# Reciprocals written as full rows and turned in one pass, in place of small reciprocals spread by fp32 products

## The chip, the cores and the metric

The kernel runs on one core of one Trainium2 chip. The metric is the device time of one execution, in microseconds (us). A change is read against the median of several executions of the kernel before.

## The reference, cut to what matters

The reference runs a convolution layer, a gated linear attention layer and a second block on a sequence of 1024 tokens and 1024 channels. Two places matter here.

The convolution mixer normalises over channels before its gate (`layer_norm` of `c`):

```python
mu = jnp.mean(xf, axis=-1, keepdims=True)
xc = xf - mu
var = jnp.mean(xc * xc, axis=-1, keepdims=True)
y = xc * lax.rsqrt(var + LN_EPS) * g + b
```

The second block has a causal attention with a softmax over keys, 8 heads of 64 channels, in blocks of 128 query rows:

```python
scores = jnp.einsum('bqhd,bkhd->bhqk', q_i, k).astype(jnp.float32) * scale
scores = scores + c_i[:, :, :, None] - c[:, :, None, :]
probs = jax.nn.softmax(scores, axis=-1).astype(v.dtype)
return jnp.einsum('bhqk,bkhd->bqhd', probs, v)
```

The kernel divides by the softmax's sum after the last product, not before it.

## The kernel before, in words

The kernel is written with explicit semaphores. Each engine (PE for products, DVE for VectorE, ACT, POOL, SP for loads) runs its own list of instructions in the written order, stage after stage, and waits where a semaphore is not yet at its count. Activations lie in SBUF with channels on the partitions and tokens along the row, so a number that belongs to a token or to a query row has to be made the same on all partitions before it can multiply such a tile.

**The attention stage** (functions `attn_tensor`, `attn_scalar`, `attn_vector`, `attn_pool`) goes over 8 turns. A turn is a block of 128 query rows; the first turn has the last block (1024 keys), the last turn the first block (128 keys). Each turn has 8 heads, worked on in 4 pairs, so there are 32 pairs `p`, and one step of the loop serves pair `p` on PE together with older pairs. In a step, in order:

- PE: `scores(p)` (L2043) writes both heads' scores to PSUM; at the second step of the next turn `spread` (L2099); in the steps 20 to 31 two early products of the output projection (L2032, L2030; the list `FILL_AT`); `turn_probs(2p-2)` (L2072, one transpose for each block of 128 keys); `values(p-2)` (L2085); `turn_probs(2p-1)`; at the second step of a turn `pooled` (L2108).
- DVE: `reduce(2p)` (L2227, adds the decay to the scores and takes the row's minimum; it waits for `scores(p)`), `keep(2p-2)` (L2237, copies the second half of the turned probabilities out of PSUM), `reduce(2p+1)`, at the first step of the next turn `sums` (L2242), `keep(2p-1)`, at the second step `leave` (L2248, L2251).
- ACT: `leave(2p-2)` (L2167, copies the first half of the turned probabilities), at the second step `keep_spread` (L2173), two `probs` (L2054, the exponential, whose accumulator gives the row's sum), `leave(2p-1)`, and some larger casts.

`turn_probs(s)` waits until the first `s` probabilities have been copied out of PSUM by ACT (`prob_left`) and by DVE (`prob_kept`), since all use the same two banks.

**The row sums.** The exponentials of a turn leave 8 sums for each query row in 8 columns of the tile `stat`. DVE inverts them in place (`sums`, L2242, 128x8). PE then makes each of the 8 columns into 64 equal rows (`spread`, L2099): an fp32 product whose stationary operand is the column repeated 64 times and whose moving operand is the identity. The result in PSUM bank 7 has channels on partitions and query rows along the row. ACT copies it to `sums_bc` (L2173) and DVE multiplies the attention output with it (L2248). PE's list has `spread` right behind `scores(p)` and ahead of the early products and `turn_probs(2p-2)`.

**The deviations.** After the convolution the tokens are in four chunks. For the chunks 1 to 3 PE sums the squares, turns the sums into columns of `stat`, ACT takes the root, DVE inverts the 1 or 3 columns (`inverse`, L785), and `variance_spread` (L773) makes each column into a 128x128 block by an fp32 product with the identity: 7 in all. DVE multiplies with that block (L799). Around it PE runs products that are already possible (L956, L967), and ACT runs roots (L838) and, after the last root, a table load and the SiLUs (L844).

In the code below `at(name, shape, offset, type)` names a region of SBUF; two names may share a region.

Of the kernel before, what the change touches and what calls it, by code (L numbers as in the profile page):

```python
# [8 lines left out]
F32R = mybir.dt.float32r  # L9
I32 = mybir.dt.int32  # L10

P = 128
# [7 lines left out]
HALF = 512  # L20
# [11 lines left out]
AH, AD = 8, 64  # L32
# [39 lines left out]
def hybrid_block(nc, I, out):  # L72
    ctx = ExitStack()
    with ctx:
        base = (nc.sbuf_base + 31) // 32 * 32

        def at(name, shape, off, dt=F32):
            return nc.alloc_sbuf_tensor_at(name, shape, dt, offset=base + off)
# [5 lines left out]
        C0 = 0  # L84
# [6 lines left out]
        Z0 = O0 + KT * T * 4  # L91

        ident_r = at("ident", [P, P], C0, F32R)
# [134 lines left out]

        PS = ctx.enter_context(nc.psum_tensor("PS", [P, 8, 512], F32))

        x_stage_t = at("x_stage_t", [P, 4, D], O0, F32R)
        silu_z_t = at("silu_z_t", [P, KT, T], O0, F32R)
        rows3_t = [silu_z_t[:, :, c:c + P] for c in (400, 528, 656)]
# [494 lines left out]
        def stat_bank(place, c):  # L728
            bank, c0 = place[c]
            return PS[:, bank, c0:c0 + CHUNKS4[c][1]]  # L730
# [39 lines left out]
        def variance_spread(pe, c):  # L770
            pe.wait_ge(centered, RSTD_LEFT[c])
            for b in range(CHUNKS4[c][1] // P):
                last = nc.tensor.matmul(stat_bank(VAR_AT, c)[:, b * P:(b + 1) * P], VAR_COLS(c)[:, b:b + 1].broadcast_to([P, P]), ident[:],  # L773
                                        start=True, stop=True)
            last.then_inc(var_ready, 1)

        def part_left(dve, c):
# [1216 lines left out]
        def row_sums(turn):  # L1994
            return stat[:, 60 + 8 * (turn % 2):68 + 8 * (turn % 2)]

        def block_cols(i):
            return slice(i * P, (i + 1) * P)
# [58 lines left out]
        def attn_tensor(pe):  # L2057
            pe.wait_ge(f_split, 4 + 2)
            pe.wait_ge(v6_left, 4 + 2 * NX)

            def scores(p):
                pair_rows(pe, p)

            def turn_probs(s):
                i, _, _ = step(s)
                a = first_blocks(i)
                pe.wait_ge(prob_ready, s + 1)
                after(pe, prob_left, s)
                after(pe, prob_kept, min(s, SPLIT))
                for kb in range(i + 1):  # L2070
                    b = kb if kb < a else 4 + kb - a
                    last = nc.tensor.transpose(blocks(4)[:, b, :].bitcast(F32R), score_t_of(s)[:, block_cols(kb)], ident_r[:])  # L2072
                last.then_inc(prob_turned, 1)

            def values(p):

                i, turn, h0 = step(2 * p)
                pe.wait_ge(prob_left, 2 * p + 2)
                pe.wait_ge(prob_kept, min(2 * p + 2, SPLIT))
                if h0 == 0 and turn > 0:  # L2080
                    pe.wait_ge(tail_dve, of_turn(turn - 1, ATTN_LEFT))
                for kb in range(i + 1):
                    for e in range(2):
                        h = h0 + e
                        ins = nc.tensor.matmul(PS[e * AD:(e + 1) * AD, 6, block_cols(h0 // 2)], v6[:, kb, h * AD:(h + 1) * AD],  # L2085
                                               prob_t[(2 * p + e) % 4][:, block_cols(kb)], start=kb == 0, stop=kb == i)
                        if kb == i:
                            ins.then_inc(pv_done, 1)

            def spread(turn):  # L2090

                pe.wait_ge(tail_dve, of_turn(turn, SUMS))
                if turn > 0:
                    pe.wait_ge(tail_dve, of_turn(turn - 1, POOL_LEFT))
                if turn > 1:
                    pe.wait_ge(tail_act, of_turn(turn - 1, SS_LEFT))
                for h in range(AH):
                    out = PS[h % 2 * AD:(h % 2 + 1) * AD, 7, block_cols(h // 2)]
                    last = nc.tensor.matmul(out, row_sums(turn)[:, h:h + 1].broadcast_to([P, AD]), ident[:], start=True, stop=True)  # L2099
                last.then_inc(tail_pe, 1)  # L2100

            def pooled(turn):
                if turn == 0:
                    pe.wait_ge(gain_in, G6 + 64)
                    pe.wait_ge(pool_ready, 4)
                pe.wait_ge(tail_act, of_turn(turn, SPREAD_LEFT))
                for g in range(4):
                    last = nc.tensor.matmul(quarter(7)[:, g, :], w_pool[:, g, :], pool_u[:, g, block_cols(row_of(turn))],  # L2108
                                            start=True, stop=True)
                last.then_inc(tail_pe, 1 if turn > 0 else 2)  # L2110

            for p in range(PAIRS + 2):
                if 0 < p < PAIRS:
                    scores(p)
                if turn_at(p, 1) is not None:
                    spread(turn_at(p, 1))
                if p in FILL_AT:
                    if p == FILL_AT[0]:
                        pe.wait_ge(w_low, 4)
                        pe.wait_ge(x_low, 1)  # L2120
                    n = 2 * (p - FILL_AT[0])
                    for e, k, m in ROW_TERMS[n:n + 2]:
                        mix_product(0, e, k, m, 1)
                if 1 <= p <= PAIRS:
                    turn_probs(2 * p - 2)
                if p >= 2:
                    values(p - 2)
                if 1 <= p <= PAIRS:
                    turn_probs(2 * p - 1)
                if turn_at(p, 1) is not None:  # L2130
                    pooled(turn_at(p, 1))
                if turn_at(p, 2) is not None and turn_at(p, 2) > 0:
                    square_sums(pe, turn_at(p, 2) - 1)
# [83 lines left out]
        def attn_vector(dve):  # L2217
            dve.wait_ge(cum_in, 16)

            def reduce(s):  # L2220
                i, _, h = step(s)
                n = (i + 1) * P
                dve.wait_ge(score_done, s + 1)
                dve.wait_ge(mask_done, s + 1)
                after(dve, prob_turned, s - 3)

                nc.vector.tensor_tensor_reduce(score_of(s)[:, 0:n], cum_bc[:, h, 0:n], banks(2 * (s % 2), 2, n), 1.0, BIG,  # L2227
                                               ALU.add, ALU.min, low_score(s)).then_inc(score_ready, 1)

            def keep(s):  # L2230
                i, _, _ = step(s)
                a, n = first_blocks(i) * P, (i + 1) * P
                if i == 0:
                    return
                dve.wait_ge(prob_turned, s + 1)
                after(dve, pv_done, 2 * (s // 2 - 1))
                nc.vector.tensor_copy(prob_t[s % 4][:, a:n], PS[:, 5, 0:n - a]).then_inc(prob_kept, 1)  # L2237

            def sums(turn):

                dve.wait_ge(prob_ready, (turn + 1) * AH)
                nc.vector.reciprocal(row_sums(turn), row_sums(turn)).then_inc(tail_dve, 1)  # L2242

            def leave(turn):
                cols = block_cols(row_of(turn))
                dve.wait_ge(tail_act, of_turn(turn, SPREAD_LEFT))
                dve.wait_ge(pv_done, (turn + 1) * AH)
                nc.vector.tensor_tensor(mix_t[:, 0:4, cols], quarter(6), sums_bc[:].rearrange("p (k q) -> p k q", k=4), ALU.mult)\  # L2248
                    .then_inc(tail_dve, 1)
                dve.wait_ge(tail_pe, of_turn(turn, POOLED))  # L2250
                nc.vector.tensor_tensor(mix_t[:, 4:8, cols], quarter(7),  # L2251
                                        pool_gain[:].rearrange("p (k o) -> p k o", o=1).broadcast_to([P, 4, P]), ALU.mult)\
                    .then_inc(tail_dve, 1)

            for p in range(PAIRS + 2):
                if p < PAIRS:
                    reduce(2 * p)
                if 1 <= p <= PAIRS:
                    keep(2 * p - 2)
                if p < PAIRS:  # L2260
                    reduce(2 * p + 1)
                if turn_at(p, 0) is not None:
                    sums(turn_at(p, 0))
                if 1 <= p <= PAIRS:
                    keep(2 * p - 1)
                if turn_at(p, 1) is not None:
                    leave(turn_at(p, 1))
                if turn_at(p, 2) is not None and turn_at(p, 2) >= 4:
                    weights_low(dve, nc.vector, turn_at(p, 2))
            weights_low(dve, nc.vector, NX - 1)  # L2270
# [1012 lines left out]
```

## Time and profile before

| | us |
|---|---|
| median of 3 runs | 2139.09 (2138.34 to 2140.31) |
| time of the profiled execution | 2136.45 |
| its span in the profile | 2134.7 |
| PE busy | 2104.7 (99% of the span) |
| DVE busy | 1267.3 (59%) |
| ACT busy | 810.6 (38%) |
| POOL busy | 1035.2 (48%) |

The span runs from the first to the last instruction of the profiled execution; its time is 1.75 us longer. PE is busy nearly all the time by this count, which takes a matmul from its issue to its modelled end, so the count hides short waits. The attention stage lies at about 1114 to 1250 us, and the deviations are spread at 314 to 326 us.

### The profile page before, as it was taken

How to read it: one execution, taken by the hardware profiler on the slowest of the kernel's cores; microseconds unless marked ns; L12 is line 12 of the kernel's file. 1: busy time of each engine (PE TensorE's matmuls, PEld its weight loads, DVE VectorE, ACT ScalarE, POOL GpSimd, SP SyncE). 2: the span in 40 equal slices, each digit the busy share in tenths (PEclk: the TensorE clock that was granted, in tenths of full speed). 3: DMA queues.
4: the chain of work that ended last, by engine and by line, in shares of the span. 5: the costliest groups of instructions: out<-in, count | busy, mean ns of one | idle time of the engine just before them, and what ended most of it. 6: DMA issues, size and time to landing. Idle time of an engine off the chain costs nothing.

```text
span 2134.7 us, 31643 instructions
## 1 busy us (share of the span) xinstructions
PE 2104.7 (99%) x12176; PEld 1820.7 (85%) x12176; DVE 1267.3 (59%) x1674; ACT 810.6 (38%) x1324; POOL 1035.2 (48%) x723
## 2 busy tenths in 40 slices
PE   8999999999999999999999999999999999999999
PEld 8999977899999998888787778888888888888787
DVE  4899988900049976640016645866656666666854
ACT  3454554112158852210226754432222222222453
POOL 3789941142256745022295630265556556555700
PEclk9999999999999999999999999999999999999999
DMA  4111123411100024221302022111111111111421
GB/s 162 41 40 40 61 79 90 127 56 40 41 21 1 1 82 146 89 70 40 119 1 85 2 99 109 50 47 52 49 59 55 44 49 59 59 39 49 178 72 56
DMA packets 128729, 136.65 MB, mean 64 GB/s; under 512 B 7054, under 2 KB 113294, under 8 KB 128492
## 3 DMA queue, kind: packets, MB, share of 16 engines
q1 hardware_dynamic: 128620, 135.11, 19.2%
q8 instruction: 79, 1.29, 0.2%
q14 instruction: 30, 0.25, 0.0%
HBM read 118.29 MB, written 16.81 MB: 63 GB/s over the span
## 4 chain that ended last, share of the span: by engine, by line
PE 82%; DVE 7%; POOL 4%; issue 3%; ACT 3%; DMA 1%; POOLq 0%; SPq 0%; ACTq 0%; DVEq 0%
PE PS L390 43%; PE PS L2700 18%; PE PS L2032 4%; POOL side_sum L622 2%; PE PS L2043 2%; PE PS L2085 2%; PE PS L2413 2%; PE PS L1323 1%; PE PS L1356 1%; PE PS L2072 1%; PE PS L440 1%; POOL wl L366 1%; PE PS L429 1%; PE PS L1741 1%; ACT glu L844 1%
## 5 line engine op out<-in xcount | busy, mean ns | idle before, releaser
L2899 DVE TENSOR_TENSOR ff_acc<-ff_acc,PS 128x512 f32<-128x512 f32 x320 | 216.4, 685 | 185.4 <-PE PS L390 184.8
L390 PE MATMUL PS<-xh,wh 128*128 128x352 f32 (+2 forms) x944 | 288.2, 337 | 1.3 <-ACT silu_z L577 1.1
L390 PE MATMUL PS<-xl,wh 128*128 128x352 f32 (+2 forms) x944 | 286.5, 335 | 0.0
L390 PE MATMUL PS<-xh,wl 128*128 128x352 f32 (+2 forms) x944 | 285.9, 334 | 0.0
L2615 POOL TENSOR_TENSOR xl<-raw,xh 128x512 fp32r<-128x512 f32 x120 | 164.6, 1380 | 136.6 <-ACT xh L2752 136.6
L674 DVE SCALAR_TENSOR_TENSOR PS<-glu,conv_vec,PS 128x1040 f32<-128x1040 f32 (+2 forms) x196 | 228.5, 1236 | 1.1
L390 PE MATMUL PS<-wh,xh 128*128 128x256 f32 (+1 forms) x712 | 207.9, 316 | 1.5 <-ACT r_silu L1629 0.6
L390 PE MATMUL PS<-wl,xh 128*128 128x256 f32 (+1 forms) x712 | 206.8, 314 | 0.0
L390 PE MATMUL PS<-wh,xl 128*128 128x256 f32 (+1 forms) x712 | 206.4, 314 | 0.0
L390 PEld LDWEIGHTS PS<-xh,wh 128*128 128x128 f32 x944 | 175.2, 189 | 9.4 <-issue 1.3
L390 PEld LDWEIGHTS PS<-xl,wh 128*128 128x128 f32 x944 | 175.0, 188 | 8.0
L390 PEld LDWEIGHTS PS<-xh,wl 128*128 128x128 f32 x944 | 174.9, 188 | 7.7
L371 POOL CAST wh<-raw 128x2048 fp32r<-128x2048 f32 x15 | 28.5, 1897 | 294.7 <-PE PS L390 142.9
L2752 ACT CAST xh<-raw 128x512 fp32r<-128x512 f32 x120 | 72.4, 619 | 238.2 <-PE PS L2700 141.6
L366 POOL TENSOR_TENSOR wl<-raw,wh 128x2048 fp32r<-128x2048 f32 x29 | 134.3, 4631 | 26.3 <-ACT wh L362 25.1
L390 PEld LDWEIGHTS PS<-wh,xh 128*128 128x128 f32 x712 | 132.7, 188 | 11.2 <-ACT v_meta L1234 1.1
L390 PEld LDWEIGHTS PS<-wh,xl 128*128 128x128 f32 x712 | 134.1, 188 | 9.1
L390 PEld LDWEIGHTS PS<-wl,xh 128*128 128x128 f32 x712 | 133.8, 188 | 9.2
L2607 POOL TENSOR_TENSOR raw<-raw 128x512 f32<-128x512 f32 x80 | 115.2, 1441 | 50.7 <-DMA raw<-in_w_ffn_up_dram 44.7
L390 PE MATMUL PS<-dnh,ffh 128*128 128x512 f32 x336 | 131.1, 390 | 0.3 <-ACT ff_acc L2763 0.3
L390 PE MATMUL PS<-dnh,ffl 128*128 128x512 f32 x336 | 130.8, 389 | 0.0
L390 PE MATMUL PS<-dnl,ffh 128*128 128x512 f32 x336 | 130.8, 389 | 0.0
(456 smaller groups left out, 4944.9 us busy)
## 6 DMA issues: line engine op xcount, KB each, us to landing
rows<-h_rows SPq DMA_DIRECT2D x24, 512.0 KB, 3.3
dn_raw<-in_w_ffn_down_dram SPq DMA_DIRECT2D x22, 512.0 KB, 3.5
raw<-in_gla_w_in_dram SPq DMA_DIRECT2D x10, 1024.0 KB
raw<-in_w_ffn_gate_dram SPq DMA_DIRECT2D x20, 512.0 KB
raw<-in_w_ffn_up_dram SPq DMA_DIRECT2D x20, 512.0 KB
raw<-in_conv_w_in_dram SPq DMA_DIRECT2D x16, 512.0 KB, 7.1
raw<-in_w_in_dram SPq DMA_DIRECT2D x8, 1024.0 KB
h_rows<-rows SPq DMA_DIRECT2D x16, 512.0 KB, 2.6
```

The lines of the kernel that those rows point to most:

```text
L366: nc.gpsimd.tensor_tensor(wl[slot][:], raw_of(u)[0][:], wh[slot][:].bitcast(F32), ALU.subtract).then_inc(unit_ready, 1)
L390: last = nc.tensor.matmul(out_of(c, cn), s, x[:, c0:c0 + cn], start=n == 0 and m == 0, stop=n == len(terms) - 1 and m == 2)
L622: ins = nc.gpsimd.tensor_tensor(acc[:], acc[:], tap_part[n % 3][:], ALU.add)
L674: ins = nc.vector.scalar_tensor_tensor(out=y, in0=x, scalar=w, in1=y, op0=ALU.mult, op1=ALU.add)
L2032: return nc.tensor.matmul(out, x, w[:, k, cols], start=begin, stop=end)
L2043: ins = nc.tensor.matmul(PS[:, 2 * e + c0 // 512, 0:cn], aqk[rows, k, i * P:(i + 1) * P], aqk[rows, 4 + k, c0:c0 + cn], start=True, stop=True)
L2085: ins = nc.tensor.matmul(PS[e * AD:(e + 1) * AD, 6, block_cols(h0 // 2)], v6[:, kb, h * AD:(h + 1) * AD], prob_t[(2 * p + e) % 4][:, block ...
L2607: nc.gpsimd.tensor_tensor(out, a, b, op).then_inc(pool_own.sem, 1)
L2615: nc.gpsimd.tensor_tensor(lo, OP_AT[o], hi.bitcast(F32), ALU.subtract).then_inc(unit_ready, 1)
L2700: ins = nc.tensor.matmul(PS[:, OP_BANK[o], :], s[:, k, :], x[:, k, :], start=k == 0 and m == 0, stop=k == 3 and m == 2)
L2752: nc.scalar.copy(ring(o)[0], OP_AT[o]).then_inc(unit_hi, 1)
L2899: nc.vector.tensor_tensor(x, x, PS[:, dn_bank(p, n), :], ALU.add).then_inc(dn_left, 1)
```

## The change

Three edits.

1. Two more names are given to existing regions, as fp32r: `stat_t` for `stat`, and `sums_bc_t` for `sums_bc`.
2. `variance_spread` uses a transpose of the repeated column in fp32r, into the same PSUM block, where it had an fp32 product with the identity. The seven blocks stay.
3. `sums` no longer inverts 128x8 in place. It reads each of the 8 sums 64 times and writes the inverses as a full row of 512 columns into `sums_bc`. `spread` then turns the four 128x128 blocks of that row with four transposes, where it had eight fp32 products. ACT's copy, DVE's product and the order of all lists stay.

```diff
+        stat_t = at("stat_t", [P, 96], C0 + 2272, F32R)
+        sums_bc_t = at("sums_bc_t", [P, HALF], Z0 + 32768, F32R)
...
         def variance_spread(pe, c):
             pe.wait_ge(centered, RSTD_LEFT[c])
             for b in range(CHUNKS4[c][1] // P):
-                last = nc.tensor.matmul(stat_bank(VAR_AT, c)[:, b * P:(b + 1) * P], VAR_COLS(c)[:, b:b + 1].broadcast_to([P, P]), ident[:],
-                                        start=True, stop=True)
+                col = 20 + 4 * c + b
+                last = nc.tensor.transpose(stat_bank(VAR_AT, c)[:, b * P:(b + 1) * P].bitcast(F32R), stat_t[:, col:col + 1].broadcast_to([P, P]), ident_r[:])
             last.then_inc(var_ready, 1)
...
-                for h in range(AH):
-                    out = PS[h % 2 * AD:(h % 2 + 1) * AD, 7, block_cols(h // 2)]
-                    last = nc.tensor.matmul(out, row_sums(turn)[:, h:h + 1].broadcast_to([P, AD]), ident[:], start=True, stop=True)
+                for q in range(AH // 2):
+                    last = nc.tensor.transpose(PS[:, 7, block_cols(q)].bitcast(F32R), sums_bc_t[:, block_cols(q)], ident_r[:])
                 last.then_inc(tail_pe, 1)
...
             def sums(turn):
 
                 dve.wait_ge(prob_ready, (turn + 1) * AH)
-                nc.vector.reciprocal(row_sums(turn), row_sums(turn)).then_inc(tail_dve, 1)
+                nc.vector.reciprocal(sums_bc[:].rearrange("p (h n) -> p h n", n=AD),
+                                     row_sums(turn).rearrange("p (h o) -> p h o", o=1).broadcast_to([P, AH, AD])).then_inc(tail_dve, 1)
```

## Rows read from the trace of the kernel before

**Rows 1.** The page: busy time of PE and DVE, and the chain that ended last.
```profile
PE 2104.7 (99%) x12176; PEld 1820.7 (85%) x12176; DVE 1267.3 (59%) x1674; ACT 810.6 (38%) x1324; POOL 1035.2 (48%) x723
...
PE 82%; DVE 7%; POOL 4%; issue 3%; ACT 3%; DMA 1%; POOLq 0%; SPq 0%; ACTq 0%; DVEq 0%
```

**Rows 2.** Busy time by stretch: PE, PEld, DVE, ACT, POOL, then granted clock.
```profile
1134.00:1155.00 21.00, 21.00 (x227) 15.66 (x225) 13.46 (x27) 14.57 (x27) 18.25 (x17) 1.00 0.06 24
1221.00:1233.00 12.00, 12.00 (x111) 8.84 (x111) 7.70 (x29) 9.06 (x30) 7.09 (x10) 1.00 0.01 1
```

**Rows 3.** Groups by shape on DVE: reciprocals, and one copy.
```profile
L2493 DVE RECIPROCAL stat<-stat 128x1 f32<-128x1 f32 x8 | 1.3, 164 | 11.6 <-ACT stat L2457 11.6
L2242 DVE RECIPROCAL stat<-stat 128x8 f32<-128x8 f32 x8 | 1.6, 198 | 1.3 <-ACT score L2054 1.3
L1636 DVE RECIPROCAL stat<-stat 128x32 f32<-128x32 f32 x1 | 0.4, 353 | 1.3 <-ACT stat L1617 1.3
L796 DVE RECIPROCAL PS<-PS 128x144 f32<-128x144 f32 x1 | 1.1, 1067 | 0.0
L2237 DVE COPY prob_t<-PS 128x512 f32<-128x512 f32 x8 | 5.5, 687 | 1.8 <-PE PS L2072 1.8
```

**Rows 4.** Timeline around the first turn's spread: start, duration, engine, line.
```profile
1134.78 0.20 DVE L2242 RECIPROCAL stat<-stat 128x8 f32<-128x8 f32 x1
1135.68 0.69 DVE L2237 COPY prob_t<-PS 128x512 f32<-128x512 f32 x1 [0.70 <-PE PS L2072]
1137.27 0.85 PEld L2099 LDWEIGHTS PS<-ident,stat 128*64 128x64 f32 x16 [0.55 <-issue]
1137.38 1.09 DVE L2227 CUSTOM_DVE_ANT_0 score<-cum_bc,PS 128x896 f32<-128x896 f32 x1 [1.01 <-PE PS L2043]
1138.30 0.66 PEld L2072 LDWEIGHTS PS<-ident,score_t 128*128 128x128 f32 x7 [0.17 <-issue]
1141.57 1.12 PE L2108 MATMUL PS<-pool_u,w_pool 128*128 128x128 f32 x8
```

**Rows 5.** Timeline, four transposes in a row and PE's next load.
```profile
1201.05 0.40 PEld L2072 LDWEIGHTS PS<-ident,score_t 128*128 128x128 f32 x4 [0.17 <-issue]
1201.39 0.52 PEld L2014 LDWEIGHTS PS<-ones_mean,sq_sum 128*128 128x128 f32 x4
```

**Rows 6.** Timeline, fourth, fifth, seventh and eighth turn: reciprocal, and what follows the spread.
```profile
1192.56 0.20 DVE L2242 RECIPROCAL stat<-stat 128x8 f32<-128x8 f32 x1
1195.35 0.39 PEld L2072 LDWEIGHTS PS<-ident,score_t 128*128 128x128 f32 x4 [0.17 <-issue]
1207.68 0.20 DVE L2242 RECIPROCAL stat<-stat 128x8 f32<-128x8 f32 x1
1210.12 0.19 PEld L2032 LDWEIGHTS PS<-mo_h,xl 128*128 128x128 f32 x1 [0.17 <-issue]
1233.52 0.20 DVE L2242 RECIPROCAL stat<-stat 128x8 f32<-128x8 f32 x1
1235.42 0.19 PEld L2032 LDWEIGHTS PS<-mo_h,xh 128*128 128x128 f32 x1 [0.17 <-issue]
1242.72 0.20 DVE L2242 RECIPROCAL stat<-stat 128x8 f32<-128x8 f32 x1 [1.31 <-ACT score L2054]
1245.69 0.59 ACT L2173 COPY sums_bc<-PS 128x512 f32<-128x512 f32 x1
1246.33 2.08 PE L2108 MATMUL PS<-pool_u,w_pool 128*128 128x128 f32 x8 [0.25 <-ACT sums_bc L2173]
```

**Rows 7.** Busy time and granted clock by stretch, end of the attention stage.
```profile
1242.00:1244.00 2.00, 0.87 (x6) 0.45 (x6) 0.20 (x1) 2.00 (x8) 1.76 (x3) 1.00 0.00 0
1244.00:1246.00 2.00, 1.89 (x21) 1.52 (x21) 0.00 (x0) 1.53 (x4) 2.00 (x1) 0.75 0.00 0
1246.00:1248.00 2.00, 1.75 (x10) 1.67 (x9) 0.69 (x1) 0.28 (x1) 0.22 (x1) 0.50 0.36 94
```

**Rows 8.** Timeline around the spread of the third chunk's deviations.
```profile
318.44 0.74 PEld L773 LDWEIGHTS PS<-ident,stat 128*128 128x128 f32 x6 [0.62 <-issue]
319.19 0.74 PEld L767 LDWEIGHTS PS<-ones_mean,var_part 128*128 128x128 f32 x6
320.25 1.28 ACT L844 ACT_TABLE_LOAD   x1
```

## The prediction, made before the changed kernel ran

> **What bounds the kernel now.** I read the page first: PE is busy 99% of the span and holds 82% of the chain that ended last; DVE is busy 59% and holds 7% of that chain [rows 1]. So time that PE gains or loses should count nearly one for one, and DVE's counts only where PE waits for it. The views by stretch say the same of the attention stage: in the stretch around the first turn's spread PE is busy 21.00 of 21 us and DVE 13.46, and in a late one 12.00 of 12 and 7.70 [rows 2]. DVE thus has some 35% of idle time there. But the timeline shows that this idle time is in pieces of 0.70 and 1.01 us between instructions that PE needs soon [rows 4], and DVE runs its list in order. The question is what one long DVE instruction does in the place of the small reciprocal.
>
> **The price of the long reciprocal.** The trace has no reciprocal of 512 columns, but it has 128x1 at 164 ns, 128x8 at 198, 128x32 at 353 and 128x144 at 1067 [rows 3]. From 1 to 32 columns this is 189/31 = 6.1 ns a column, from 32 to 144 it is 714/112 = 6.4. A copy of 512 columns takes 687 ns, 1.3 ns a column [rows 3]; the reciprocal is plainly not one column a cycle. The engine has to make 512 results even if each input is read 64 times. At 6.35 ns I get 1.07 + 368 x 0.00635 = 3.40 us, against 0.20 now: 3.2 us more on DVE in each of 8 turns. Bounds: 0.69 (the copy) and, with the steeper slope, 3.45; I take 3.40, since four points lie on one line.
>
> The Trainium skill (VectorE: DVE Perf Modes, "First, the fixed hardware budget") says that a reciprocal runs an iterative divide with a repeat count of 8. Taken as 8 cycles of 0.96 GHz a column that would be an estimated 8.3 ns and 4.4 us; the rows show about 6 cycles (6.35 ns), and they decide, but the direction is the same and speaks against a repeated input.
>
> **The price of the new spread on PE.** Now: 16 weight loads (two for each of the 8 products) from 1137.27, and the next loads at 1138.30, a slot of 1.03 us [rows 4]. Four transposes in a row hold PE 0.34 us to its next load [rows 5]; I take 0.40. Were the row ready in time, each turn would gain 0.62 us.
>
> **Where the long reciprocal lies in a turn.** It is issued at 1134.78 and would end at 1138.18, while PE wants it at 1137.27 [rows 4]. Behind it on DVE stand the copy `keep` of the old turn's last head (0.69 us) and the next `reduce`. PE waits for the reciprocal in `spread`, and behind it PE's `turn_probs` waits for that copy (`prob_kept`). First turn: copy ends at about 1134.78 + 3.32 + 0.69 = 1138.79, 0.05 for the signal, so the transposes start at 1138.84 where they started at 1138.30: +0.54. The other path, 1138.18 + 0.05 + 0.40 = 1138.63, is shorter. `reduce` starts 1.3 us later than now, at about 1138.7, and ends before ACT gets to its exponential, which stands behind PE's transposes in any case, so nothing more is added. Everything after shifts by the same amount, since each engine follows PE here.
>
> The turns get shorter (fewer keys), so the cover shrinks. Fourth turn: 1192.56 + 3.45 + 0.40 = 1196.41 against 1195.35, +1.06. Fifth: 1207.68 + 3.85 = 1211.53 against the early product at 1210.12, +1.41. Seventh: 1233.52 + 3.85 = 1237.37 against 1235.42, +1.95. Eighth: the reciprocal ends at 1246.12, the transposes reach PSUM some 0.5 us later, and ACT's copy starts at about 1246.65 against 1245.69, +0.96 [rows 6]. The second, third and sixth turn I put between their neighbours: 0.71, 0.89, 1.68. Sum: 0.54 + 0.71 + 0.89 + 1.06 + 1.41 + 1.68 + 1.95 + 0.96 = +9.2 us. PE's saving of 0.62 us a turn is already in it, since I compared starts behind the spread. POOL and SP get no new wait; their work lies behind events that shift with PE.
>
> **The deviations.** The slot of three spreads is 318.44 to 319.19, 0.75 us for 6 loads [rows 8]. Three transposes at 0.09 hold 0.27, so 0.48 less; a single one saves some 0.17. The first two spreads (one block, three blocks) stand ahead of the last root on ACT and thus of the table load at 320.25 that the SiLUs wait for; the third (0.48) lies among PE's products. DVE's reciprocal of these columns is not changed. I take -0.6 (0.17 + 0.48), with -1.2 (all three count) and 0 (DVE's later work there absorbs it) as ends.
>
> **The clock.** At the end of the attention stage PE is busy 0.87 of 2 us, then the granted clock falls to 0.75 and 0.50, the lower of the two levels, 1.2 GHz for 2.4 [rows 7]. There the eight `pooled` products take 2.08 us [rows 6] where they took 1.12 in the first turn [rows 4]. In the changed kernel PE idles about 2 us or more for the reciprocal in the fifth, sixth and seventh turn. I expect the clock to fall in one or two of these, at about 1 us each by that row (0.96): +1.2, with 0 and +4 as ends.
>
> The Trainium skill (TensorE: Matmul & The Clock Gate, Part 4) says that transposes do not count as activity for the clock. That would make the falls likelier, since the new spread is transposes where the old one was products; no row here separates the two.
>
> **Sum.** 9.2 - 0.6 + 1.2 = +9.8 us. The profiled execution (2136.45) would become about 2146.3; it is 2.6 us under the median of the runs, so for the median I give 2139.1 + 9.8 = 2148.9 us, 0.46% slower. No change that a measurement of this kernel can tell is about 0.2%, 4.3 us.
>
> **The rivals.**
> - The row costs what a copy costs (on the other side: faster). If the chip makes the repeated results at 1.3 ns a column, the reciprocal takes 0.69 us, is ready before PE wants it in every turn, and the change gives 8 x -0.62 - 0.6 = -5.6: 2133.5. For it: only that the input is the same 8 numbers. Against: the four reciprocal rows. It turns at about 2.25 us for the reciprocal (3.40 less the mean loss of 9.2/8), 4.1 ns a column. Chance 0.05.
> - The reciprocal is hidden by DVE's idle time. For it: 35% of DVE idle. Against: the copy and the spread behind it are both waited for by PE within 2.5 us in the first turn and 0.9 in the seventh. If PE had other slack that gives back most of it, +1 to +4: 2140 to 2143. Chance 0.05. A weaker form, +4.3 to +7 (2143.4 to 2146), because later waits of PE take up part: 0.08.
> - The clock falls in four or more turns, or the repeated input makes the divide dearer. Five falls: 9.2 - 0.6 + 5 = +13.6, 2152.7; a divide one us longer would give 8 more, 2157. For it: the idle times grow turn by turn. Against: no row has such short gaps with a fall but the one. Chance 0.12.
> - The forecast, +7 to +13: 0.70.
>
> **How the numbers follow.** Range 2145.0 to 2153.5: it leaves out the faster and the hidden case (0.10), some of the weaker form, and the dearest clock or divide. Faster by over 0.2%: 0.05; within 0.2%: 0.05; slower: 0.90.
>
> **What the profile of the changed kernel would show.** L2242 as 128x512 at 3.3 to 3.5 us, eight times. L2099 (under its new line number) with 4 loads a turn in 0.35 to 0.4 us. PE idle before it 0.9 us in the first turn, growing to 2.5 in the seventh, with DVE's reciprocal as the releaser. The spread of the deviations with 7 loads and not 14. The granted clock below 1.00 in some stretch between 1205 and 1240. The forecast is wrong if the reciprocal takes under 2.3 us, if PE's idle time before the spread does not grow, or if the end of the attention stage does not shift by about 9 us.

## The result, and the profile of the changed kernel

The changed kernel takes 2152.57 us (median of 4 runs, 2151.73 to 2153.59), the kernel before beside it 2138.72 us (4 runs, 2136.66 to 2140.31). The ratio is 1.0067 with a 95% interval of 1.0054 to 1.0080: 13.85 us slower, where +9.8 was forecast. The profiled execution has a span of 2150.0 us against 2134.7, 15.3 more.

First the page of the changed kernel, the busy time and the chain that ended last:

```profile
PE 2106.9 (98%) x12073; PEld 1821.5 (85%) x12073; DVE 1289.4 (60%) x1674; ACT 810.3 (38%) x1324; POOL 1035.0 (48%) x723
...
PE 76%; DVE 8%; POOL 8%; issue 4%; ACT 3%; DMA 1%; SPq 0%; POOLq 0%; DVEq 0%; ACTq 0%
```

DVE has 22.1 us more work than in [rows 1], 60% of the span against 59%; PE's busy time barely moves, and of the chain PE still has 76%, against 82%. The busy times would let one believe that nothing happened. The view of the reciprocal's line and of its instructions says otherwise (durations are minimum, median and maximum in ns; "who waited" is in us and times):

```profile
L2243 DVE RECIPROCAL sums_bc<-stat x8: 3347/3348/3353, 1134.9 to 1255.8; 128x512 f32<-128x512 f32 x8
...
  PEld PS L2100: 16.4, 8
  PE PS L2100: 13.0, 8
```

Each of the eight takes 3.35 us, and each time PE waits for it: PE idles for 13.0 us in front of the new transposes. The timeline of the first turn, and then the transposes of the fourth to eighth turn (start, duration; in brackets the engine's idle time and who ended it):

```profile
1134.89 3.35 DVE L2243 RECIPROCAL sums_bc<-stat 128x512 f32<-128x512 f32 x1
...
1138.16 0.63 DVE L2238 COPY prob_t<-PS 128x512 f32<-128x512 f32 x1
1138.30 0.39 PEld L2100 LDWEIGHTS PS<-ident,sums_bc_t 128*128 128x128 f32 x4 [1.45 <-DVE sums_bc L2243]
1138.30 0.53 PE L2100 MATMUL PS<-ident,sums_bc_t 128*128 128x128 f32 x4 [0.83 <-DVE sums_bc L2243]
1138.70 1.07 DVE L2228 CUSTOM_DVE_ANT_0 score<-cum_bc,PS 128x896 f32<-128x896 f32 x1
1138.90 0.65 PEld L2074 LDWEIGHTS PS<-ident,score_t 128*128 128x128 f32 x7 [0.22 <-issue]
...
1197.88 0.54 PE L2100 MATMUL PS<-ident,sums_bc_t 128*128 128x128 f32 x4 [1.57 <-DVE sums_bc L2243]
...
1213.94 0.53 PE L2100 MATMUL PS<-ident,sums_bc_t 128*128 128x128 f32 x4 [1.91 <-DVE sums_bc L2243]
...
1230.76 0.53 PE L2100 MATMUL PS<-ident,sums_bc_t 128*128 128x128 f32 x4 [2.16 <-DVE sums_bc L2243]
...
1245.61 0.75 PE L2100 MATMUL PS<-ident,sums_bc_t 128*128 128x128 f32 x4 [2.46 <-DVE sums_bc L2243]
...
1255.82 3.35 DVE L2243 RECIPROCAL sums_bc<-stat 128x512 f32<-128x512 f32 x1 [1.30 <-ACT score L2056]
1259.23 0.75 PE L2100 MATMUL PS<-ident,sums_bc_t 128*128 128x128 f32 x4 [1.77 <-DVE sums_bc L2243]
```

In [rows 4] the spread's slot lay from 1137.27 to 1138.30, and the next loads began at 1138.30. Now the transposes only begin there, hold PE for 0.60 us up to the next transposes at 1138.90, and these begin 0.60 later. The idle time before the spread grows from 0.83 us in the first turn to 2.46 in the seventh, as the turns get shorter. The same four transposes, 0.53 or 0.54 us in the first six turns, take 0.75 in the last two: PE's clock is down. The views by stretch show where (duration; busy us of PE, PEld, DVE, ACT, POOL; granted clock; DMA):

```profile
1206.00:1210.00 4.00, 4.00 (x41) 2.93 (x42) 2.85 (x9) 3.67 (x11) 3.92 (x8) 1.00 0.01 2
1210.00:1214.00 4.00, 2.09 (x23) 1.23 (x19) 4.00 (x5) 1.62 (x6) 2.68 (x2) 1.00 0.00 0
1214.00:1218.00 4.00, 4.00 (x29) 3.28 (x30) 1.38 (x6) 2.06 (x6) 0.91 (x2) 0.57 0.02 4
...
1226.00:1230.00 4.00, 2.60 (x24) 1.74 (x24) 3.54 (x6) 2.48 (x8) 3.74 (x5) 1.00 0.00 0
1230.00:1234.00 4.00, 3.24 (x23) 2.63 (x24) 1.81 (x7) 1.74 (x6) 0.91 (x2) 0.70 0.00 0
...
1244.00:1248.00 4.00, 2.39 (x13) 1.86 (x15) 2.10 (x6) 0.52 (x2) 0.66 (x1) 0.66 0.00 0
1248.00:1252.00 4.00, 4.00 (x21) 3.12 (x18) 1.89 (x6) 2.10 (x7) 0.00 (x0) 0.50 0.01 2
```

A stretch with PE busy 2.09 of 4 us is followed by one at 0.57; 2.60 is followed by one at 0.70; the third time the clock stays down for longer. In the kernel before there is one such fall in the stage, at its end [rows 7].

To see where the 15.3 us come from I took the starts of the reciprocals, which mark the turns. Before: 1134.78, 1156.09, 1175.53, 1192.56, 1207.68, 1221.73, 1233.52, 1242.72. After: 1134.89, 1156.68, 1176.68, 1194.47, 1210.53, 1227.36, 1242.20, 1255.82. The difference of the intervals is what a turn lost; the last one runs to the end of the span (891.98 and 894.18 us).

| turn | 1 | 2 | 3 | 4 | 5 | 6 | 7 | 8 | sum |
|---|---|---|---|---|---|---|---|---|---|
| lost, us | 0.48 | 0.56 | 0.76 | 0.94 | 2.78 | 3.05 | 4.42 | 2.20 | 15.2 |
| forecast without the clock | 0.54 | 0.71 | 0.89 | 1.06 | 1.41 | 1.68 | 1.95 | 0.96 | 9.2 |

The first four turns are as forecast, each 0.06 to 0.15 us under it. The last four lost 12.45 where 6.0 was forecast: these are the turns in which the clock is down. The rest, 0.1 us, lies ahead of the first turn, where the deviations should have given 0.6; but single executions scatter by more than that there. In the executions shown below the first turn's reciprocal starts anywhere from 1134.38 to 1137.75, so the views of turns are compared by their intervals, and the deviations by a view of their own.

### The profile page after: what moved, and what is told of

The parts are those of the page before. It is cut to its first block, busy times and chain, and to the rows that moved or that the text cites. A ratio compares the mean times of both kernels' runs of the same rounds, so it can differ in the third digit from the quotient of the medians.

```text
span 2150.0 us, 31437 instructions
## 1 busy us (share of the span) xinstructions
PE 2106.9 (98%) x12073; PEld 1821.5 (85%) x12073; DVE 1289.4 (60%) x1674; ACT 810.3 (38%) x1324; POOL 1035.0 (48%) x723
## 4 chain that ended last, share of the span: by engine, by line
PE 76%; DVE 8%; POOL 8%; issue 4%; ACT 3%; DMA 1%; SPq 0%; POOLq 0%; DVEq 0%; ACTq 0%
PE PS L392 40%; PE PS L2702 18%; PE PS L2034 3%; POOL side_sum L624 2%; PE PS L2415 2%; PE PS L1325 1%; PE PS L1358 1%; PE PS L442 1%; POOL wl L368 1%; DVE sums_bc L2243 1%; PE PS L431 1%; PE PS L1743 1%; POOL pool_tmp L2288 1%; PE PS L2087 1%; ACT glu L846 1%
## 5 line engine op out<-in xcount | busy, mean ns | idle before, releaser
L676 DVE SCALAR_TENSOR_TENSOR PS<-glu,conv_vec,PS 128x1040 f32<-128x1040 f32 (+2 forms) x196 | 228.4, 1232 | 1.1
```

Of the source, the lines that this page charges most:

```text
L676: ins = nc.vector.scalar_tensor_tensor(out=y, in0=x, scalar=w, in1=y, op0=ALU.mult, op1=ALU.add)
```

## The experiments

My theory: the loss is the time that PE waits for the long reciprocal, and in the short turns PE's clock falls on top. Rivals: the deviations cost or give something; the transposes are the dearer part; the clock is a small term, and something else makes the late turns dearer. All kernels compute the whole reference. Those with filler make, besides, fp32 products of the identity with itself whose result nobody reads: each is two loads and two matmuls, and eight in a row hold PE's loads for 1.86 us, 0.23 us each.

**One part of the change each.** `e1_conv_alone` has only the new `variance_spread`, `e2_attn_alone` only the long reciprocal and the transposes in `spread`.

> Only the deviations' spread is changed; the attention stage is as before. Theory A (the gain goes into a new wait): the seven transposes take half the loads, but PE's next product behind the third chunk's spread waits for VectorE's copy of the next chunk's partial sums, so the time stays within 1 us of before. Theory B (the forecast's step): PE's list ahead of the last root gets shorter by 0.6 us and the kernel with it, 2138.1. Theory C: the deviations carry part of the loss, 1 us or more slower.

> Only the attention edit, the deviations' spread as before. Theory A: the whole loss is here, +13 to +15 us. Rival: part of it comes from the deviations or from an interplay of both, then +11 us or less.

Measured beside a median before of 2137.79: 2137.49 for the deviations alone, ratio 0.9996 (0.9987 to 1.0005), and 2152.39 for the attention alone, 1.0064 (1.0051 to 1.0078). The whole loss is the attention part, and the deviations bring nothing that shows; by itself the interval, from -2.8 to +1.1 us, would leave room for the forecast 0.6. The timeline decides it. First the deviations alone, then the kernel before:

```profile
318.89 0.29 PEld L776 LDWEIGHTS PS<-ident,stat_t 128*128 128x128 f32 x3 [0.62 <-issue]
...
319.03 0.56 DVE L783 COPY var_part<-PS 128x384 f32<-128x384 f32 x1 [1.08 <-PE PS L763]
...
319.64 0.74 PEld L769 LDWEIGHTS PS<-ones_mean,var_part 128*128 128x128 f32 x6 [0.46 <-DVE var_part L783]
...
328.85 0.73 PE L392 MATMUL PS<-wh,xh 128*128 128x512 f32 x2 [0.68 <-DVE xl L812]
```

```profile
318.58 0.56 DVE L781 COPY var_part<-PS 128x384 f32<-128x384 f32 x1 [1.07 <-PE PS L761]
...
328.39 0.73 PE L390 MATMUL PS<-wh,xh 128*128 128x512 f32 x2 [0.26 <-DVE xl L810]
```

The three transposes do hold PE for only 0.29 us, but the next loads still begin 0.75 us after them, exactly the slot of [rows 8]. The gap is now a wait for DVE's copy of `var_part`, which ends at 319.59. In the kernel before that copy ends at 319.14, 0.05 us ahead of the same loads: PE's work filled the time, and what PE saved it now waits. The last spread does give PE some 0.4 us, but behind it PE waits for DVE's `xl`, 0.68 us where it waited 0.26, and that product starts 0.46 us later than before, as did the work ahead of the deviations (0.4 us).

`e2_attn_alone` also shows that the falls of the clock are not tied to certain turns. Its fourth turn has the same idle time of 1.57 us before the transposes as the changed kernel's, and there the clock falls (the two views are its transposes and its stretch of 4 us behind them):

```profile
1198.72 0.55 PE L2100 MATMUL PS<-ident,sums_bc_t 128*128 128x128 f32 x4 [1.57 <-DVE sums_bc L2243]
```

```profile
1202.00:1206.00 4.00, 4.00 (x30) 2.95 (x31) 2.82 (x7) 1.95 (x4) 0.37 (x1) 0.78 0.02 4
```

Turn by turn it lost 0.48, 0.57, 0.75, 2.43, 2.81, 3.06, 3.08 and, up to the end of the span, 1.76 us: 14.9 in all, as much as the changed kernel, otherwise divided.

**A small reciprocal, and the row by a copy.** `e3_small_reciprocal_then_copy` keeps the four transposes and leaves out the slow form:

```
-                nc.vector.reciprocal(<row of 512>, <8 sums, each read 64 times>).then_inc(tail_dve, 1)
+                dve_own.step(dve, nc.vector.reciprocal(row_sums(turn), row_sums(turn)))
+                nc.vector.tensor_copy(<row of 512>, <8 sums, each read 64 times>).then_inc(tail_dve, 1)
```

> The reciprocal is 128x8 in place as before, then VectorE copies it to the full row, and PE turns the row with the four transposes. Theory A (the loss is the long reciprocal alone, and the four transposes by themselves are worth 0.6 us a turn): the copy takes 0.3 to 0.7 us and is done before PE wants it in every turn, so the kernel gets faster than before by 8 x 0.6 = 4.8 us, 2134. Rival (the transposes cost more than they look, for instance through the clock): same as before or slower. The middle case, 2137 to 2139: in the late turns the copy comes just too late.

Measured: 2139.14, ratio 1.0004 (0.9995 to 1.0013). The loss is gone, so it was the long reciprocal and not the transposes; but there is no gain either, where theory A had 2134. The first three turns each take 0.7 us less than before (intervals 20.61, 18.77, 16.34 against 21.31, 19.44, 17.03), which is the slot saved; the sixth and seventh take 0.46 and 1.22 more, and from the eighth reciprocal to the end of the span it is 1.09 more, with the clock at 0.84, 0.50 and 0.80 in the stretches from 1244, 1248 and 1252. (`dve_own.step` makes DVE wait for its own small reciprocal.) The view of the copy's line, and its timeline in the first and the seventh turn:

```profile
L2244 DVE COPY sums_bc<-stat x8: 426/1815/2508, 1137.7 to 1245.2; 128x512 f32<-128x512 f32 x8
```

```profile
1137.67 0.43 DVE L2244 COPY sums_bc<-stat 128x512 f32<-128x512 f32 x1
...
1234.62 2.35 POOL L2309 TENSOR_TENSOR xl<-mix_t,xh 128x1024 fp32r<-128x1024 f32 x1
...
1234.74 2.51 DVE L2244 COPY sums_bc<-stat 128x512 f32<-128x512 f32 x1
...
1237.30 0.22 PEld L2100 LDWEIGHTS PS<-ident,sums_bc_t 128*128 128x128 f32 x2 [2.05 <-DVE sums_bc L2244]
```

The same copy takes 0.43 us alone and 2.51 beside an instruction of POOL; it ends 0.28 us after POOL's does. In the fourth to sixth turn it is the same beside the making of `xl` (1.78 to 2.06 us), and in the second beside that of `mix_sq` (1.85): each time the copy ends 0.27 to 0.29 us after POOL's instruction. In all of these POOL's instruction had begun first. In the eighth turn the copy began first, 0.02 us ahead of the making of `sq_sum`; there it took 0.43 us, and POOL's instruction 0.99 where the same one took 0.72 to 0.79 in the other turns. So by these rows the one that begins later waits. The long reciprocal shows nothing of the kind, 3347 to 3353 ns in all turns, with POOL making `xl` beside it in most of them, in the fourth and fifth turn begun ahead of it. The Trainium skill (GPSIMD Engine Reference, "Specifications") says that GpSimd shares its SBUF interfaces with VectorE and collides with its instructions in a 2-port mode or with two SBUF inputs; VectorE: DVE Perf Modes ("Mode 2×_2P") says that copies from SBUF to SBUF are among the operations that can use such a mode. The trace agrees that the two collide, 0.43 against 2.51; no run here shows that the mode is the reason.

**The row by ACT.** `e5_row_made_by_act`: the small reciprocal, and ACT copies the row, behind its last copy of the old turn.

```
+            def make_row(turn):
+                act.wait_ge(tail_dve, of_turn(turn, SUMS))
+                nc.scalar.copy(<row of 512>, <8 inverse sums, each read 64 times>).then_inc(row_made, 1)
```

> Reciprocal 128x8 in place on VectorE, ScalarE copies it to the full row behind its last copy of the step, four transposes on PE. Theory A (the four transposes are worth 0.6 to 0.7 us a turn wherever the row is there in time, and VectorE's copy was late only because it stretched beside GpSimd's long instructions): ScalarE's copy takes 0.6 us in every turn. It is in time in the first five turns and up to 0.7 us late in the last, so the kernel gets 2 to 4 us faster than before, 2134 to 2136. Rival: ScalarE's own queue is pushed back and gives the gain back, same as before. It would be the first version that beats both kernels.

> The kernel of the fifth run again beside the two others, to tell its small gain from none: -1.8 us if the first measurement holds, 0 if it was the scatter.

Measured: 2135.49 beside 2137.28, ratio 0.9993 (0.9984 to 1.0002); the second time 2134.87 beside 2137.02, 0.9992 (0.9983 to 1.0001). Both medians are lower, by 1.8 and 2.2 us, and neither interval excludes no change. ACT's copy in the first and the seventh turn, and PE's loads behind it:

```profile
1136.38 0.62 ACT L2173 COPY sums_bc<-stat 128x512 f32<-128x512 f32 x1
...
1137.25 0.39 PEld L2101 LDWEIGHTS PS<-ident,sums_bc_t 128*128 128x128 f32 x4 [0.54 <-ACT sums_bc L2173]
...
1231.08 2.37 POOL L2315 TENSOR_TENSOR xl<-mix_t,xh 128x1024 fp32r<-128x1024 f32 x1
...
1231.86 0.63 ACT L2173 COPY sums_bc<-stat 128x512 f32<-128x512 f32 x1
...
1232.55 0.22 PEld L2101 LDWEIGHTS PS<-ident,sums_bc_t 128*128 128x128 f32 x2 [0.83 <-ACT sums_bc L2173]
```

ACT's copy takes 0.61 to 0.64 us in all turns, beside POOL's making of `xl` too. In the first turn it ends at 1137.00 and PE's matmuls run through; in the seventh PE waits for it. Turn by turn the intervals are 0.70, 0.69, 0.08, 0.46, 0.42 and 0.18 us shorter than before, and 0.03 longer in the seventh: 2.5 us in seven turns, not 7 x 0.62 = 4.3. From the eighth reciprocal to the end of the span it takes 0.92 us more than before, which eats more than a third of that; the granted clock is 0.50 from 1242 to 1248 us.

**How much is the clock?** `e4_long_reciprocal_pe_kept_busy` and `e6_filler_cut_to_the_gap` are the changed kernel with filler in front of PE's wait for the row in the last five turns, so that PE doesn't idle there; the first has 10, 13, 15, 17 and 14 products, the second 5, 7, 8, 9 and 6.

```
+                if turn >= 3:
+                    for n in range(WARM[turn]):
+                        nc.tensor.matmul(PS[:, 7, 0:P], ident[:], ident[:], start=True, stop=True)
                 pe.wait_ge(tail_dve, of_turn(turn, SUMS))
```

> The changed kernel, but in the turns 4 to 8 PE runs 10 to 17 small fp32 products of the identity into the same PSUM bank ahead of its wait for the reciprocal; the spread overwrites their result. Theory A (of the loss of 13.9 us some 6 us are the clock that falls after PE's idle time): the granted clock stays at 1.00 in the turns 5 to 7 and the kernel is 4 to 6 us faster than the changed one, +8 to +10 over before. Rival 1 (the waits alone make the loss, the clock is a side effect): no gain, +13 to +15. Rival 2: the filler itself delays the spread, and it is slower than the changed kernel.

> The changed kernel with the filler of the run before cut to the idle time measured in the changed kernel: 5, 7, 8, 9 and 6 products at 0.25 us in the turns 4 to 8, where it had 10 to 17, which overshot the gap. Theory A (the clock's falls cost some 5 to 6 us of the 13.9): the clock stays at 1.00 from 1206 to 1245 us, the fifth to seventh turn lose 1.4, 1.6 and 1.9 us and no more, and the kernel comes to +8.5 to +10 over before. Rival (the falls cost nothing by themselves): +13 to +14, with the clock up.

The first took 2152.53 beside 2137.79, ratio 1.0066 (1.0053 to 1.0080): nothing won. Its clock is 1.00 in the stretches of 4 us from 1206, 1214, 1232 and 1244, but the filler ran on beyond the gap: its 17 products of the seventh turn hold PE for 4.06 us, where the gap was 2.46. Its fourth to seventh turn are 1.58, 2.23, 2.69 and 3.11 us longer than before, and the eighth, up to the end of the span, 3.60. What the clock costs cannot be read from it. The second took 2145.95 beside 2137.28, ratio 1.0038 (1.0025 to 1.0052), 8.7 us over its base where the attention part alone was 14.6 over its own. Its stretches:

```profile
1214.00:1218.00 4.00, 3.85 (x40) 3.28 (x39) 2.72 (x9) 2.10 (x7) 0.93 (x2) 1.00 0.01 4
1232.00:1236.00 4.00, 4.00 (x34) 3.14 (x36) 3.00 (x10) 3.34 (x13) 1.26 (x3) 1.00 0.00 0
1244.00:1248.00 4.00, 3.92 (x32) 2.63 (x30) 2.17 (x7) 3.02 (x10) 0.00 (x0) 1.00 0.03 6
1252.00:1256.00 4.00, 3.64 (x21) 3.55 (x21) 2.33 (x1) 1.65 (x6) 2.36 (x1) 0.57 0.00 0
```

The clock stays up except at the very end, and the turns lose 0.46, 0.56, 0.76, 0.94, 1.33, 1.55, 1.88 and, up to the end of the span, 0.95 us, 8.4 in all. The first four are those of the changed kernel, and the last four are what was forecast without the clock. So the falls cost 6.8 us by the turns (15.2 - 8.4), and by the medians 5.9 against the attention part alone (14.6 - 8.7) or 5.2 against the changed kernel (13.85 - 8.67). The slowest run with this filler, 2146.77, is 3.98 us under the fastest of `e2_attn_alone`, 2150.75.

**The long row in the first four turns only.** `e7_long_row_in_first_four_turns` goes back to the products of the kernel before in the last four.

> The long reciprocal and the four transposes in the first four turns alone, the small reciprocal and the eight products in the last four. Theory A (the loss grows as the turns get shorter, by cover and by clock): +2.5 to +3.5 us, a fifth of the whole loss. Rival (each turn loses the same): half of it, +7.

Measured: 2138.53 beside 2137.28, ratio 1.0005 (0.9996 to 1.0014). Its first four intervals are 21.78, 20.01, 17.79 and 16.08 us, 2.76 more than before in all, and the next three 14.04, 11.79 and 9.19, as before. Here a turn with the long row harms no later one; no fall of the clock came in the fourth turn of this execution. The median moved by 1.25 us; 2.76 is still within the interval, so this run fixes the price of four turns by its trace alone.

**Filler in the last turn.** In the last turn the kernel before has a fall of its own [rows 7]. `e8_before_with_filler_in_last_turn` puts 3 and 2 products ahead of the last two `turn_probs`; `e9_row_by_act_and_filler` does the same, with 3 more ahead of the last spread, in the kernel in which ACT makes the row.

> The kernel before, with five small products of the identity in the last step of the attention stage (three ahead of its first turn of probabilities, two ahead of its second), into a PSUM bank that is idle there. Theory A (the fall of the clock at the end of the stage comes from PE's two idle gaps of 0.8 us and costs 1.5 to 2 us): the granted clock stays at 1.00 from 1244 to 1248 us and the kernel is 1.5 to 2 us faster, 2135.5. Rival (the fall costs nothing, or the filler delays what it stands before): same as before or slower.

> The version with ScalarE's row (fifth run) and the same filler, with three more products ahead of the last spread. Theory A: both gains add, 2 us of the row and 1.5 to 2 us of the clock, 2133.5 to 2134, clear of the kernel before. Rival: the row's copy on ScalarE is what the last turn waits for, and the filler brings nothing there, -2.

Measured beside 2137.02: 2135.76, ratio 0.9993 (0.9984 to 1.0002), and 2134.06, 0.9982 (0.9972 to 0.9991). The stretches of the second:

```profile
1240.00:1244.00 4.00, 3.97 (x33) 3.00 (x30) 0.71 (x5) 3.52 (x12) 2.90 (x3) 1.00 0.00 0
1244.00:1248.00 4.00, 3.33 (x25) 2.65 (x24) 1.58 (x3) 2.03 (x4) 1.47 (x1) 1.00 0.31 86
```

The clock no longer falls there, in either of the two. By itself that is 1.3 us, too little to be told from nothing by its interval; in the trace the time from the eighth reciprocal to DVE's next one behind the stage (1253.31 before, 1251.74 here) is 1.1 us shorter than before, and to the end of the span 0.7. Where ACT makes the row the same filler shortens the time from the eighth reciprocal to the end of the span by 1.9 us (891.04 against the 892.90 of `e5_row_made_by_act`). This is the one version that is clearly faster than the kernel before, by 3.0 us between the medians and by 0.18% in the ratio, and the one with the lowest median of all that ran; `e10_row_made_by_act_again`, measured beside it, is 0.8 us above it, with runs that overlap.

## Why the prediction was right, and where its sizes were off

- **The direction and the mechanism** were right: a long DVE instruction in front of a product that PE wants soon, repeated eight times. `e2_attn_alone` carries the loss alone, and `e3_small_reciprocal_then_copy`, with the same transposes, doesn't have it. The size was not: the forecast proper, +7 to +13 us, missed 13.85.
- **The price of the reciprocal**: 3.40 us forecast, 3.35 measured. The line through four shorter rows [rows 3] held out to 512 columns: (3.348 - 1.067)/368 is 6.2 ns a column, not the 6.35 assumed. Reading each sum 64 times makes it no cheaper; the copy's price as a lower bound is refuted. The measured 6.2 ns speak against the 8.3 ns that the prediction estimated from the Trainium skill (VectorE: DVE Perf Modes, "First, the fixed hardware budget").
- **The slot of the spread**: 0.40 us forecast, up to the next loads 0.60 in the first turn, since those wait for the copy `prob_kept` behind the reciprocal; this is the gate that the prediction took for the first turn (1138.84 forecast, 1138.90 seen). That forecast used 3.32 us up to the copy without a reason, where 3.40 was assumed elsewhere; with 3.40 it would have been 1138.92 and +0.62. Measured, the copy starts 3.27 us after the reciprocal does.
- **The turns without the clock**: +9.2 forecast, 8.4 in `e6_filler_cut_to_the_gap`. Each term is right within 0.15 us; that the loss grows as the turns get shorter is right too.
- **The clock** is the term that was mis-sized: +1.2 forecast, with +4 as its upper end, 5.2 to 6.8 measured. I expected a fall in one or two turns at 1 us. It fell in three (fifth, sixth, seventh) and was down again in the eighth, in `e2_attn_alone` in the fourth too, and a turn with a fall lost 1.2 to 2.5 us more than the same turn in `e6_filler_cut_to_the_gap` (2.78 - 1.33 = 1.45, 1.50, 2.54, 1.25). So both the number of falls and the price of one were too low, the number more so. The row that I priced it by [rows 7] was at the end of the stage, where PE is idle part of the time (1.75 of 2 us busy at 0.50); in the middle it is busy throughout (4.00 of 4 at 0.57), which would make a fall dearer there. That is a reading of the rows; no run tests it by itself. So the case of many falls (+13.6), at 0.12, came nearest to the measured 13.85, not the likeliest one; the time lay within the range only because the range reached into that case.
- **The deviations** were off too: -0.6 forecast, nothing measured, the end named at 0. The saved time became waits for `var_part` and for `xl`. The prediction asked which engines stand behind the spread, but not when DVE is done with what PE wants next.
- **DVE's idle time** hid only a part: the eight reciprocals got 25.2 us longer together, and PE waited 13.0 us for them. That it would not hide the whole was right. The rival of the cheap row (under 2.25 us) could be tried with another engine: a row in 0.43 or 0.62 us gives 0.7 us a turn in the first turns, close to the 0.62 reckoned. But it is lost again in the short ones, where even 0.6 us on ACT is on PE's path, and where the last turn's fall of the clock gets longer.

## What to carry to other kernels

Spread a small result after the slow operation, not before it: here an input read with a repeat still cost the slow price for each element of the output. When an engine that is busy 60% of the time gets a longer instruction, look at when its next consumer wants the result, not at its share; and where a change makes the main engine idle for 1.6 to 2.5 us again and again, count the clock as well, by a stretch with as much work behind the gap. A saving on the main engine is worth only what lies up to the next input that is late, so look up that input's end first.

## What the runs showed of the hardware

- A DVE copy from SBUF to SBUF of 128x512 took 0.43 us alone and up to 2.51 beside the POOL instruction that makes `xl`, 1.85 beside the one that makes `mix_sq`, and ended 0.27 to 0.29 us after that instruction; where the copy began first, POOL's instruction got longer instead (0.99 us for 0.72 to 0.79); ACT's copy of the same data stayed at 0.61 to 0.64, DVE's reciprocal at 3.35.
- A DVE reciprocal of 128x512, each input read 64 times, took 3.35 us, 6.2 ns a column from 144 columns on.
- PE's clock fell to the lower level after idle gaps of 1.91, 2.16 and 2.46 us with PE otherwise at work, and stayed at full speed when products of the identity filled the gap. After a gap of 1.57 us it fell in one execution and not in another. Whether the transposes themselves count for the clock, as the prediction asked, no run here separates: the filler was products.
- A fall cost 1.2 to 2.5 us a turn in the last four turns of the changed kernel; avoiding the one at the end of the stage gave 1.3 us by the medians (not told from nothing) and 0.7 to 1.1 in the trace of the kernel before, 1.9 where ACT makes the row.
